# The first up products of a ConvFFN, made in the stage before it

## The chip, the cores and the metric

One core of one Trainium2 chip runs the whole kernel. The metric is the device time in microseconds (us); the median of three runs of the kernel before is 2347.77. The profile names the engines PE (TensorE, its matmuls), PEld (its weight loads), DVE (VectorE), ACT (ScalarE), POOL (GpSimd) and SP (SyncE). Each has its own queue of instructions, and they meet through semaphores.

## The reference, cut to what matters

One layer of a streaming encoder over 1024 prompt rows and 64 sample rows, width 1024, in float32. After attention and a gated merge come the two parts that this case is about:

```
x   = x + rms_norm(merged @ w_o, g_post_mix)
up  = rms_norm(x, g_pre_ffn) @ w_up                 # 1024 -> 2 x 2816, gate and value
buf = concatenate([conv_prev, up], axis=1)
conv = b_conv + sum(w_conv[i] * buf[:, i:i + t] for i in range(3))
gate, val = split(conv, 2)
x   = x + rms_norm((gelu(gate) * val) @ w_down, g_post_ffn)
```

## The kernel before

The kernel works in stages, each a function with a block of instructions for each engine. At the end of a stage all engines meet in a barrier, the stage's semaphores are cleared by POOL, a second barrier follows, and the next stage starts. Matrix products in float32 are made as three passes over high and low parts (`three_passes`, lines 166 to 170), so every operand is split first: a high part in a rounded type, and a low part that is the rest.

**The output stage** (`phase_output`) goes over nine tiles of rows, m = 0 to 8 (the ninth is the 64 sample rows). For a tile, PE makes `product(m)`, 48 matmuls into PSUM. ACT sums squares, DVE scales (`y_scaled`), adds x and writes `h2`, the normalized input of the FFN. PE turns h2 by eight transposes (`turn(m)`, line 1636). ACT then copies the high part of the result into `h2T` (named mergedT in the profile, line 1651) and DVE makes the low part (`lo(m)`, line 1689). Products run two tiles ahead of the transposes. DVE writes the low part of tile m - 2 within its work on tile m, and those of the last two tiles at the end. PSUM has eight banks: `p7_ps` takes four (two tiles), `p7_psT` the other four. POOL splits the first two pieces of w_up (gate and value, each 128 output features) early in this stage, into slots 0 and 1 of the weight ring.

**The FFN stage** (`phase_ffn`) has 22 steps f of 128 features. The 1092 columns of h2T (rows and gaps) are cut in three chunks of 364. In a step:

- PE: `up(f, b, 0)`, the gate half, three chunks of 24 matmuls; `down(f - 1)`, 54 matmuls in 18 shares; `up(f, b, 1)`, the value half. Step 0 has no down product. The first down product stands in step 1, between its gate and value halves. The chunks go to four banks of PSUM in turn.
- ACT: copies each chunk out of PSUM (line 1866, `up_taken`), begins the convolution of a half (line 1874), gelu (line 1879), and the high part of the hidden values (line 1881).
- DVE: adds the shares of the last step to the accumulator (line 1906), small copies (lines 1912 to 1914) and two multiply-adds for each half (line 1917), the product of gate and value (line 1933), the low part `hid_lo` (line 1935). `down` waits for `hid_lo`. At the stage's start it clears the accumulator (line 1942).
- POOL: splits the weights of the steps to come, n = 3f + kind (gate, value, w_down), a high part (line 148) and a low part (line 151). Six slots; a split of an up piece waits until the products that read the slot two steps before are made (line 1796).
- SP: loads the raw weights (line 142) into two buffers, one for even and one for odd n; a load waits until the split two before it is done.

Steps 0 and 1 are written out; the others run in a loop of 10 passes, two steps each.

Of the kernel before, what the change touches and what calls it, by code (L numbers as in the profile page):

```python
# [25 lines left out]
ACT = mybir.ActivationFunctionType  # L26
F32 = mybir.dt.float32
# [3 lines left out]
P = 128  # L31
D = 1024
KT = D // P
# [14 lines left out]
EPS = 1e-6  # L48
SCALE = DH ** -0.5
RSQRT_MAGIC = float(0x5F3759DF)  # L50


def rows(m):

    return P if m < TILES - 1 else DEC


def col(m):

    return GAP + m * P if m < TILES - 1 else SCOL  # L60
# [155 lines left out]
def build_layer(nc, a, o):  # L216

    base = (nc.sbuf_base + 63) // 64 * 64
    small = Place(nc, base, 3072)
    region = COLS * KT * 4 * 2  # L220
    r0 = base + 3072
    r1 = r0 + region
    rf = r1 + region
    f_size = nc.sbuf_usable_end - rf
    ident = small("ident", [P, P])
    par = small("par", [P, 512])
    d = Scratch(nc)
# [12 lines left out]
    phase_sample_attention(nc, a, d, ident, yaT, r1, region + f_size)  # L240
    phase_merge(nc, a, d, ybT, mgT, rf, f_size)
    ffn_place = Place(nc, rf, f_size)
    ffn_ring = Weights.buffers("p8", FFN_SLOTS, ffn_place, ffn_place)
    phase_output(nc, a, ident, mgT, d.x2, ffn_ring, r0, region, rf, f_size)
    phase_ffn(nc, a, o, ident, par, mgT, d.x2, ffn_ring, ffn_place.at, r0, region, rf, f_size)


def feature_part(nc, out, ring, slot, pair, chunk, first=0, count=3 * KT):
# [1292 lines left out]

def phase_output(nc, a, ident, mgT, x2_dram, ffn_ring, r0, r0_size, rf, rf_size):


    w_o = a["w_o"][0].rearrange("(k p) c -> p k c", p=P)
# [1 line left out]
    h2T = mgT  # L1549
    RAW = 4  # L1550
    LAG = 2
    with ExitStack() as ctx:
        s = Sems(nc, ctx, "p7")
# [3 lines left out]
        next_raw, next_hi, next_lo = ffn_ring  # L1557
# [16 lines left out]
        ss = f("p7_ss", [P, 2, 2])  # L1574
        rstd = f("p7_rstd", [P, 2, 2])
        tmp = f("p7_tmp", [P, 2, 2])
        ps = ctx.enter_context(nc.psum_tensor("p7_ps", [P, 2, D], F32))
        psT = ctx.enter_context(nc.psum_tensor("p7_psT", [P, 2, KT, P], F32))
        with nc.Block() as block:

            @block.sync
# [33 lines left out]
            @block.tensor  # L1615
            def _(pe):
                def product(m):
                    for c in range(2):
                        if m >= 2 and c == 0:
                            pe.wait_ge(s("y_scaled"), m - 1)  # L1620
                        for k in range(KT):
                            slot, at = 4 * c + k // 2, (k % 2) * 512
                            if m == 0 and k % 2 == 0:
                                pe.wait_ge(s("w_lo"), slot + 1)
                            last = three_passes(
                                nc, ps[0:rows(m), m % 2, c * 512:(c + 1) * 512], mgT[0][:, k, col(m):col(m) + rows(m)],
                                mgT[1][:, k, col(m):col(m) + rows(m)], w_hi[:, slot, at:at + 512],
                                w_lo[:, slot, at:at + 512], k == 0, k == KT - 1)
                    last.then_inc(s("product"), 1)

                def turn(m):
                    pe.wait_ge(s("h2_ready"), m + 1)
                    if m >= 2:
                        pe.wait_ge(s("h2T_lo"), m - 1)
                    for k in range(KT):
                        last = nc.tensor.transpose(psT[:, m % 2, k, 0:rows(m)], h2[0:rows(m), m % 2, k * P:(k + 1) * P],
                                                   ident[0:rows(m), 0:rows(m)])
                    last.then_inc(s("h2_turned"), 1)

                product(0)  # L1640
                product(1)
                for m in range(TILES):
                    if m + 2 < TILES:
                        product(m + 2)
                    turn(m)

            @block.scalar
            def _(act):
                def hi(m):
                    act.wait_ge(s("h2_turned"), m + 1)  # L1650
                    nc.scalar.activation(h2T[0][:, :, col(m):col(m) + rows(m)], psT[:, m % 2, :, 0:rows(m)],
                                         ACT.Copy).then_inc(s("h2T_hi"), 1)

                for n in range(8):
                    act.wait_ge(s(f"raw_ready{n % RAW}"), 16 * (n // RAW + 1))
                    nc.scalar.activation(w_hi[:, n, :], w_raw[n % RAW], ACT.Copy).then_inc(s("w_hi"), 1)
                act.wait_ge(s("ss_set"), 1)
                for m in range(TILES):
                    r = rows(m)
                    act.wait_ge(s("product"), m + 1)  # L1660
                    if m >= 2:
                        act.wait_ge(s("h2_ready"), m - 1)
                    nc.scalar.activation(junk[0:r, :], ps[0:r, m % 2, :], ACT.Square,
                                         accum_out=ss[0:r, m % 2, 0:1]).then_inc(s("squares"), 1)
                    act.wait_ge(s("squares"), 2 * m + 1)
                    if m >= LAG:
                        hi(m - LAG)
                    act.wait_ge(s("x2_ready"), m + 1)
                    nc.scalar.activation(junk[0:r, :], y[0:r, m % 2, :], ACT.Square,
                                         accum_out=ss[0:r, m % 2, 1:2]).then_inc(s("squares"), 1)  # L1670
                    act.wait_ge(s("squares"), 2 * m + 2)
                for m in range(TILES - LAG, TILES):
                    hi(m)

            @block.vector
            def _(dve):
# [9 lines left out]
                def lo(m):  # L1686
                    c = slice(col(m), col(m) + rows(m))
                    dve.wait_ge(s("h2T_hi"), m + 1)
                    nc.vector.tensor_tensor(h2T[1][:, :, c], psT[:, m % 2, :, 0:rows(m)], h2T[0][:, :, c].bitcast(F32),
                                            ALU.subtract).then_inc(s("h2T_lo"), 1)  # L1690

                for m in range(TILES):
# [5 lines left out]
                    nc.vector.scalar_tensor_tensor(out=y[0:r, b, :], in0=ps[0:r, b, :], scalar=rstd[0:r, b, 0:1],  # L1698
                                                   in1=g_post[0:r, :], op0=ALU.mult, op1=ALU.mult).then_inc(s("y_scaled"), 1)
                    dve.wait_ge(s("y_scaled"), m + 1)  # L1700
                    dve.wait_ge(s(f"x_ready{b}"), 16 * (m // 2 + 1))
# [11 lines left out]

def phase_ffn(nc, a, o, ident, par, h2T, x2_dram, ffn_ring, ffn_ring_end, r0, r0_size, rf, rf_size):

# [10 lines left out]
    with ExitStack() as ctx:  # L1728
# [18 lines left out]
        psU = ctx.enter_context(nc.psum_tensor("p8_psU", [P, BANKS, 512], F32))  # L1747
# [18 lines left out]
        with nc.Block() as block:  # L1766
# [25 lines left out]
            def _(pool):  # L1792
                def step(f, b, first):
                    for kind in range(AHEAD if first else 0, 3):
                        if kind < 2:
                            pool.wait_ge(s("up"), f * CHUNKS + (kind + 1) * NCH)
                        else:
                            pool.wait_ge(s("share"), f * SHARES + SHARES)
                        n = 3 * b + kind

                        ring.split_one(pool, f * 3 + kind, (f - b) * 3 // 2 + n // 2, n, n % 2)
# [14 lines left out]
            def _(pe):  # L1816
# [23 lines left out]
                                         ring.lo[:, slot, w], True, True).then_inc(s("share"), 1)  # L1840

                def step(f, b, first):
                    up(f, b, 0)
                    if not first:
                        down(f - 1, 1 - b)
                    up(f, b, 1)

                pe.sem_inc(s("up"), 2 * CHUNKS)
# [8 lines left out]
            @block.scalar  # L1857
            def _(act):
                def step(f, b, first):
                    for kind in range(2):  # L1860
                        for c in range(NCH):
                            n = kind * NCH + c
# [14 lines left out]
                        if kind == 0:  # L1877
                            act.wait_ge(s("conv"), f * 2 + 3)
                            nc.scalar.activation(cv[0][:, GAP:COLS], cv[0][:, GAP:COLS], ACT.Gelu_apprx_tanh).then_inc(s("gelu"), 1)  # L1879
                    act.wait_ge(s("hid"), f + 2)  # L1880
                    nc.scalar.activation(hid_hi[:, GAP:COLS], cv[0][:, GAP:COLS], ACT.Copy).then_inc(s("hid_hi"), 1)

                act.sem_inc(s("up_taken"), BANKS)  # L1883
# [106 lines left out]
```

## Time and profile before

| | |
|---|---|
| three runs | 2345.87, 2347.77, 2348.48 us |
| the profiled execution, its own time | 2350.03 us |
| its span, first to last instruction | 2348.1 us |
| mean granted TensorE clock | 0.961 of full speed |
| PE busy | 2163.6 us, 92% |
| DVE, ACT, POOL busy | 1306.8, 746.6, 858.4 us |
| PE busy in 1393.00 to 1491.35 (output stage) | 98.35 of 98.35 us, clock 1.00 |
| PE busy in 1491.35 to 1504.17 | 1.11 of 12.82 us, clock 0.70 |
| PE busy in 1504.17 to 1542.77 (up products of steps 0 and 1) | 38.59 of 38.60 us, clock 0.92 |
| PE busy in 1542.77 to 2295.10 | 752.33 of 752.33 us, clock 1.00 |

Times in the profile are microseconds from the start of the span. A busy share is that of an engine's own instructions; the matmuls overlap, so that one of 0.33 us can follow another after 0.17 us. In a timeline, the bracket at the end of a line tells how long the engine had been idle and which instruction released it.

### The profile page before, as it was taken

The page shows a single profiled execution, that of the slowest core. Times are in us where ns is not written, and L with a number is a line of the kernel's source. Part 1 is how long each engine was busy: PE and PEld are TensorE (multiplying, and loading weights), DVE is VectorE, ACT ScalarE, POOL GpSimd, SP SyncE. Part 2 cuts the span into 40 slices and gives each one's busy share as a digit, 9 for nine tenths or more (in the row PEclk, how much of TensorE's full clock was granted, in tenths as well). Part 3 has the DMA queues.
Part 4 walks back from the last instruction along what each step waited for, and adds up shares of the span by engine and source line. Part 5 has one row for each costly group of instructions (what it writes and reads, how often), then busy time and mean ns, then how long its engine had stood idle before and what let it go on. Part 6 is the DMA issues. An engine that isn't in the chain of part 4 may idle for free. (4 is left out here: it accounts for less than half of the span.)

```text
span 2348.1 us, 33627 instructions
## 1 busy us (share of the span) xinstructions
PE 2163.6 (92%) x12884; PEld 2056.2 (88%) x12884; DVE 1306.8 (56%) x1719; ACT 746.6 (32%) x1429; POOL 858.4 (37%) x485
## 2 busy tenths in 40 slices
PE   6999999995999999937996989899999999999993
PEld 6999999995999999927996978699999999999992
DVE  5054220001787788745563547666767667677666
ACT  3211102232677777723432122221121211212122
POOL 2335334442555455432543310324233242332404
PEclk9999999998999999968997989899999999999996
DMA  5124224456555554346645443211111111111104
GB/s 169 46 83 145 84 75 160 160 162 169 131 129 133 144 128 124 77 140 165 173 136 183 122 151 95 81 45 46 36 54 36 45 47 33 54 44 36 45 0 162
DMA packets 289092, 237.39 MB, mean 101 GB/s; under 512 B 50950, under 2 KB 265430, under 8 KB 288982
## 3 DMA queue, kind: packets, MB, share of 16 engines
q1 hardware_dynamic: 280240, 222.24, 33.0%
q10 hardware_dynamic: 7510, 9.19, 1.3%
q0 software_dynamic: 1232, 4.46, 0.5%
q8 instruction: 74, 1.21, 0.2%
q14 instruction: 36, 0.29, 0.0%
HBM read 168.51 MB, written 67.33 MB: 100 GB/s over the span
## 5 line engine op out<-in xcount | busy, mean ns | idle before, releaser
L148 POOL TENSOR_SCALAR p_w_hi<-p_w_raw 128x1024 fp32r<-128x1024 f32 x136 | 167.7, 1233 | 896.0 <-PE p_psD L170 418.5
L995 DVE TENSOR_TENSOR_SCAN p_rest<-p_rest 128x896 f32<-128x896 f32 (+7 forms) x128 | 218.5, 1718 | 304.2 <-ACT p_rest L947 303.5
L151 POOL TENSOR_TENSOR p_w_lo<-p_w_raw,p_w_hi 128x1024 fp32r<-128x1024 f32 x136 | 356.7, 2622 | 11.3
L168 PE MATMUL p_psU<-mergedT_lo,p_w_hi 128*128 128x364 f32 x1056 | 347.1, 329 | 2.7 <-ACTq L1883 2.7
L170 PE MATMUL p_psU<-mergedT_hi,p_w_lo 128*128 128x364 f32 x1056 | 347.9, 329 | 0.0
L169 PE MATMUL p_psU<-mergedT_hi,p_w_hi 128*128 128x364 f32 x1056 | 347.5, 329 | 0.0
L257 PE MATMUL p_psB<-hT_lo,p_w_hi 128*128 128x364 f32 x960 | 318.8, 332 | 2.4 <-issue 2.4
L257 PE MATMUL p_psB<-hT_hi,p_w_lo 128*128 128x364 f32 x960 | 316.5, 330 | 0.0
L257 PE MATMUL p_psB<-hT_hi,p_w_hi 128*128 128x364 f32 x960 | 315.9, 329 | 0.0
L1906 DVE TENSOR_TENSOR p_acc<-p_psD,p_acc 128x512 f32<-128x512 f32 (+1 forms) x396 | 273.4, 691 | 46.6 <-PE p_psD L170 45.3
L823 POOL TENSOR_TENSOR p_weights<-p_weights,p_rest 128x895 f32<-128x895 f32 (+7 forms) x128 | 159.8, 1254 | 200.5 <-DVE p_rest L995 198.6
L168 PEld LDWEIGHTS p_psU<-mergedT_lo,p_w_hi 128*128 128x128 f32 x1056 | 199.3, 189 | 5.0 <-POOLq L132 2.9
L169 PEld LDWEIGHTS p_psU<-mergedT_hi,p_w_hi 128*128 128x128 f32 x1056 | 199.3, 189 | 0.8
L170 PEld LDWEIGHTS p_psU<-mergedT_hi,p_w_lo 128*128 128x128 f32 x1056 | 199.2, 189 | 0.0
L257 PEld LDWEIGHTS p_psB<-hT_lo,p_w_hi 128*128 128x128 f32 x960 | 181.4, 189 | 3.2 <-issue 2.6
L532 ACT ACTIVATE p_line<-p_psB 128x364 f32<-128x364 f32 x117 | 55.5, 474 | 403.1 <-PE p_psB L257 403.1
L257 PEld LDWEIGHTS p_psB<-hT_hi,p_w_hi 128*128 128x128 f32 x960 | 181.2, 189 | 0.0
L257 PEld LDWEIGHTS p_psB<-hT_hi,p_w_lo 128*128 128x128 f32 x960 | 181.1, 189 | 0.0
L168 PE MATMUL p_psD<-p_w_lo,p_hid_hi 128*128 128x512 f32 (+1 forms) x396 | 156.5, 395 | 9.4 <-issue 9.4
L169 PE MATMUL p_psD<-p_w_hi,p_hid_hi 128*128 128x512 f32 (+1 forms) x396 | 157.1, 397 | 0.0
L170 PE MATMUL p_psD<-p_w_hi,p_hid_lo 128*128 128x512 f32 (+1 forms) x396 | 156.3, 395 | 0.0
L1879 ACT ACTIVATE p_conv_gate<-p_conv_gate 128x1090 f32<-128x1090 f32 x22 | 24.6, 1117 | 367.5 <-DVE p_conv_gate L1917 367.5
(208 smaller groups left out, 4364.5 us busy)
## 6 DMA issues: line engine op xcount, KB each, us to landing
p_w_raw<-in_w_up SPq DMA_DIRECT2D x44, 512.0 KB, 3.8
p_w_raw<-in_w_in SPq DMA_DIRECT2D x40, 512.0 KB, 4.0
p_w_raw<-in_w_down SPq DMA_DIRECT2D x22, 512.0 KB, 3.5
p_kT_hi<-k_hi_scratch SPq DMA_DIRECT2D x32, 256.0 KB, 4.5
p_kT_lo<-k_lo_scratch SPq DMA_DIRECT2D x32, 256.0 KB, 5.1
p_w_raw<-in_w_gate SPq DMA_DIRECT2D x16, 512.0 KB, 4.1
p_raw_k<-in_cache_sb_k SPq DMA_DIRECT2D x8, 1024.0 KB, 7.9
p_raw_v<-in_cache_sb_v SPq DMA_DIRECT2D x8, 1024.0 KB, 6.7
```

Of the source, the lines that this page charges most:

```text
L148: self.nc.gpsimd.tensor_scalar(self.hi[:, slot, :], self.raw[:, parity, :], 1.0, 0.0, ALU.mult, ALU.add).then_inc(self.split, 1)
L151: self.nc.gpsimd.tensor_tensor(self.lo[:, slot, :], self.raw[:, parity, :], self.hi[:, slot, :].bitcast(F32), ALU.subtract).then_inc(self. ...
L168: nc.tensor.matmul(out, stat_hi, mov_lo, start=first, stop=False)
L169: nc.tensor.matmul(out, stat_hi, mov_hi, start=False, stop=False)
L170: return nc.tensor.matmul(out, stat_lo, mov_hi, start=False, stop=last)
L257: last = nc.tensor.matmul(out[:, 0:CH], stat[:, slot, w], mov[:, k, c], start=(at == 0), stop=(at == 3 * KT - 1))
L532: nc.scalar.activation(line_of(n)[:, c * CH:(c + 1) * CH], psB[:, q % 3, 0:CH], func).then_inc(s("line"), 1)
L823: nc.gpsimd.tensor_tensor(wt[:, b % 6, 0:n - 1], wt[:, b % 6, 0:n - 1], rest[:, b % 4, 1:n], ALU.mult).then_inc(s("weights"), 1)
L995: nc.vector.tensor_tensor_scan(src, src, src, 1.0, ALU.mult, ALU.bypass).then_inc(s("scanned"), 1)
L1879: nc.scalar.activation(cv[0][:, GAP:COLS], cv[0][:, GAP:COLS], ACT.Gelu_apprx_tanh).then_inc(s("gelu"), 1)
L1906: nc.vector.tensor_tensor(acc[0:r, m, w], psD[0:r, share_bank(b, n), :], acc[0:r, m, w], ALU.add).then_inc(s("added"), 1)
```

## The change

PE makes four of the six up chunks of step 0 in the output stage. In `UP_FIRST` the chunks of step 0 get an order of their own: gate 0, gate 1, value 0, value 1, then gate 2, value 2. The first two are made ahead of the transposes of the last tile, the next two behind them. They write into a PSUM tensor `ps_up` of four banks that both stages share: in the output stage its banks 0 and 1 are the product's second buffer, banks 2 and 3 the transposes' second buffer. The early chunks therefore wait: the first two for `y_scaled` of tile 7, the other two for the low part of tile 7. The FFN stage starts with a count of four chunks made, makes the last two, and ACT begins the convolutions of both halves of step 0 only behind the sixth copy. POOL's wait for the gate slot becomes one for the fifth chunk of two steps before, in place of the third, in every step. The semaphore that tells that the early chunks are made has a group of its own, which is given back behind the FFN stage.

```diff
+UP_FIRST = [(0, 0), (0, 1), (1, 0), (1, 1), (0, 2), (1, 2)]
+UP_EARLY = 4
...
+    with ExitStack() as both:
+        early = Sems(nc, both, "early")
+        ps_up = both.enter_context(nc.psum_tensor("ps_up", [P, 4, 512], F32))
...
-        ps = ctx.enter_context(nc.psum_tensor("p7_ps", [P, 2, D], F32))
-        psT = ctx.enter_context(nc.psum_tensor("p7_psT", [P, 2, KT, P], F32))
+        ps = [ctx.enter_context(nc.psum_tensor("p7_ps", [P, D], F32)), ps_up[:, 0:2, :].rearrange("p b c -> p (b c)")]
+        psT = [ctx.enter_context(nc.psum_tensor("p7_psT", [P, KT, P], F32)), ps_up[:, 2:4, :].rearrange("p b (k c) -> p (b k) c", c=P)]
...
+                def up(n):
+                    kind, c = UP_FIRST[n]
+                    pe.wait_ge(s("next_split"), 2 * kind + 2)
+                    pe.wait_ge(s("h2T_lo"), 3 * c + 3)
+                    if n < 2:
+                        pe.wait_ge(s("y_scaled"), TILES - 1)
+                    else:
+                        pe.wait_ge(s("h2T_lo"), TILES - 1)
+                    cols = slice(c * CH, (c + 1) * CH)
+                    for k in range(KT):
+                        w = slice(k * P, (k + 1) * P)
+                        last = three_passes(nc, ps_up[:, n, 0:CH], next_hi[:, kind, w], next_lo[:, kind, w],
+                                            h2T[0][:, k, cols], h2T[1][:, k, cols], k == 0, k == KT - 1)
+                    last.then_inc(early("up_opened"), 1)
...
                     if m + 2 < TILES:
                         product(m + 2)
+                    if m == TILES - 1:
+                        up(0)
+                        up(1)
                     turn(m)
+                for n in range(2, UP_EARLY):
+                    up(n)
...
-                            pool.wait_ge(s("up"), f * CHUNKS + (kind + 1) * NCH)
+                            pool.wait_ge(s("up"), f * CHUNKS + (CHUNKS - 1, CHUNKS)[kind])
...
                 def step(f, b, first):
+                    if first:
+                        pe.wait_ge(early("up_opened"), UP_EARLY)
+                        pe.sem_inc(s("up"), UP_EARLY)
+                        for n in range(UP_EARLY, CHUNKS):
+                            kind, c = UP_FIRST[n]
+                            pe.wait_ge(s("up_taken"), n + 1)
...
+                            last.then_inc(s("up"), 1)
+                        return
...
+                def first_step():
+                    for n, (kind, c) in enumerate(UP_FIRST):
+                        act.wait_ge(s("up"), n + 1 + 2 * CHUNKS)
+                        if c == 0:
+                            act.wait_ge(s("conv"), kind + 1)
+                        nc.scalar.activation(x[kind][:, c * CH:(c + 1) * CH], psU[:, n % BANKS, 0:CH], ACT.Copy).then_inc(s("up_taken"), 1)
+                    act.wait_ge(s("up_taken"), CHUNKS + BANKS)
+                    act.wait_ge(s("hid_lo"), 1)
+                    act.wait_ge(s("hid"), 1)
+                    for kind in range(2):
+                        at = kind * FT
+                        nc.scalar.activation(cv[kind][:, GAP:COLS], x[kind][:, GAP:COLS], ACT.Identity,
+                                             scale=par[:, PAR["w_conv2"] + at:PAR["w_conv2"] + at + 1],
+                                             bias=par[:, PAR["b_conv"] + at:PAR["b_conv"] + at + 1]).then_inc(s("conv_begun"), 1)
+                    act.wait_ge(s("conv"), 3)
+                    nc.scalar.activation(cv[0][:, GAP:COLS], cv[0][:, GAP:COLS], ACT.Gelu_apprx_tanh).then_inc(s("gelu"), 1)
+                    act.wait_ge(s("hid"), 2)
+                    nc.scalar.activation(hid_hi[:, GAP:COLS], cv[0][:, GAP:COLS], ACT.Copy).then_inc(s("hid_hi"), 1)
```

## Rows read from the trace of the kernel before

**Rows 1.** PE's waits from 1480 us on: us in total, times, longest.

```profile
PE p_psD L168 <- issue: 9.4, 1, 9.4
PE p_psT L1636 <- DVE p_h L1709: 9.0, 1, 9.0
PE p_psU L168 <- ACTq L1883: 2.7, 1, 2.7
```

**Rows 2.** Busy us of each engine in a stretch, clock, DMA.

```profile
1567.00:2295.00 728.00, 728.00 (x3963) 674.33 (x3961) 505.56 (x600) 144.72 (x200) 227.77 (x112) 1.00 0.13 39
```

**Rows 3.** PE's timeline: start, us, instruction, [idle before, releaser].

```profile
1489.44 1.91 PE L1636 MATMUL p_psT<-ident,p_h 128*128 128x128 f32 x16
...
1500.34 1.11 PE L1636 MATMUL p_psT<-ident,p_h 64*128 64x64 f32 x8 [8.99 <-DVE p_h L1709]
1504.17 0.65 PE L168 MATMUL p_psU<-mergedT_lo,p_w_hi 128*128 128x364 f32 x1 [2.72 <-ACTq L1883]
...
1542.77 0.39 PE L168 MATMUL p_psD<-p_w_lo,p_hid_hi 128*128 128x512 f32 x1
```

**Rows 4.** DVE's timeline at the end of the output stage.

```profile
1500.21 1.21 DVE L1689 TENSOR_TENSOR mergedT_lo<-p_psT,mergedT_hi 128x1024 fp32r<-128x1024 f32 x1
1502.12 0.69 DVE L1689 TENSOR_TENSOR mergedT_lo<-p_psT,mergedT_hi 128x512 fp32r<-128x512 f32 x1 [0.70 <-ACT mergedT_hi L1651]
```

**Rows 5.** Busy us in two stretches (columns as in rows 2).

```profile
1504.10:1510.10 6.00, 5.92 (x20) 5.96 (x21) 4.09 (x1) 0.00 (x0) 2.46 (x2) 0.50 0.58 175
...
2295.10:2304.50 9.40, 0.00 (x0) 0.00 (x0) 5.72 (x7) 2.88 (x3) 0.00 (x0) 0.68 0.84 318
```

**Rows 6.** ACT's timeline, step 0 of the FFN.

```profile
1515.09 0.47 ACT L1866 ACTIVATE p_up_gate<-p_psU 128x364 f32<-128x364 f32 x1 [3.52 <-PE p_psU L170]
1519.06 0.48 ACT L1866 ACTIVATE p_up_gate<-p_psU 128x364 f32<-128x364 f32 x1 [3.50 <-PE p_psU L170]
1519.57 1.30 ACT L1874 ACTIVATE p_conv_gate<-p_up_gate,par 128x1090 f32<-128x1090 f32 x1
```

**Rows 7.** PE's queue, two lines that open the FFN: duration ns, first and last start.

```profile
L1848 PEldq EVENT_SEMAPHORE  x1: 51/51/51, 1503.7 to 1503.7; - x1
...
L1821 PEldq EVENT_SEMAPHORE  x1: 51/51/51, 1504.1 to 1504.1; - x1
```

**Rows 8.** POOL's timeline, first splits of the FFN.

```profile
1507.55 1.04 POOL L148 TENSOR_SCALAR p_w_hi<-p_w_raw 128x1024 fp32r<-128x1024 f32 x1 [11.14 <-DMA p_w_raw<-in_w_down]
...
1512.15 2.39 POOL L151 TENSOR_TENSOR p_w_lo<-p_w_raw,p_w_hi 128x1024 fp32r<-128x1024 f32 x1
1515.09 1.05 POOL L148 TENSOR_SCALAR p_w_hi<-p_w_raw 128x1024 fp32r<-128x1024 f32 x1 [0.55 <-issue]
...
1531.20 1.05 POOL L148 TENSOR_SCALAR p_w_hi<-p_w_raw 128x1024 fp32r<-128x1024 f32 x1 [3.20 <-PE p_psU L170]
```

**Rows 9.** DVE's timeline, value half and low split of step 0.

```profile
1534.94 2.75 DVE L1917 SCALAR_TENSOR_TENSOR p_conv_val<-p_up_val,par,p_conv_val 128x1090 f32<-128x1090 f32 x2
...
1540.27 1.29 DVE L1935 TENSOR_TENSOR p_hid_lo<-p_conv_gate,p_hid_hi 128x1090 fp32r<-128x1090 f32 x1 [1.18 <-ACT p_hid_hi L1881]
```

**Rows 10.** DVE's timeline near 1593 us.

```profile
1593.39 3.33 DVE L1917 SCALAR_TENSOR_TENSOR p_conv_gate<-p_up_gate,par,p_conv_gate 128x1090 f32<-128x1090 f32 x1 [0.15 <-DVE p_up_gate L1914]
1596.87 1.90 DVE L1917 SCALAR_TENSOR_TENSOR p_conv_gate<-p_up_gate,par,p_conv_gate 128x1090 f32<-128x1090 f32 x1 [0.15 <-DVE p_conv_gate L1917]
```

**Rows 11.** POOL's timeline near 1593 us.

```profile
1593.17 2.40 POOL L151 TENSOR_TENSOR p_w_lo<-p_w_raw,p_w_hi 128x1024 fp32r<-128x1024 f32 x1
1595.54 2.09 POOL L148 TENSOR_SCALAR p_w_hi<-p_w_raw 128x1024 fp32r<-128x1024 f32 x1
1597.71 3.32 POOL L151 TENSOR_TENSOR p_w_lo<-p_w_raw,p_w_hi 128x1024 fp32r<-128x1024 f32 x1
```

**Rows 12.** SP's timeline: the loads behind the boundary.

```profile
1504.17 7.29 SPq L142 DMA_DIRECT2D p_w_raw<-in_w_up  x2
```

**Rows 13.** The last release of semaphores: first and last start.

```profile
L87 POOLq DRAIN  x1: 107/107/107, 2347.5 to 2347.5; - x1
```

More of the change, by code:

```diff
@@ L243, in build_layer @@
     ffn_ring = Weights.buffers("p8", FFN_SLOTS, ffn_place, ffn_place)
[L244 to L245 removed]
+    with ExitStack() as both:
+        early = Sems(nc, both, "early")
+        ps_up = both.enter_context(nc.psum_tensor("ps_up", [P, 4, 512], F32))
+        phase_output(nc, a, ident, mgT, d.x2, ffn_ring, early, ps_up, r0, region, rf, f_size)
+        phase_ffn(nc, a, o, ident, par, mgT, d.x2, ffn_ring, early, ps_up, ffn_place.at, r0, region, rf, f_size)
 def feature_part(nc, out, ring, slot, pair, chunk, first=0, count=3 * KT):
@@ L1540, in _, with phase_output @@
                 lo(len(ORDER) - 1)
-def phase_output(nc, a, ident, mgT, x2_dram, ffn_ring, r0, r0_size, rf, rf_size):
+def phase_output(nc, a, ident, mgT, x2_dram, ffn_ring, early, ps_up, r0, r0_size, rf, rf_size):
     w_o = a["w_o"][0].rearrange("(k p) c -> p k c", p=P)
@@ L1625, in product @@
                             last = three_passes(
-                                nc, ps[0:rows(m), m % 2, c * 512:(c + 1) * 512], mgT[0][:, k, col(m):col(m) + rows(m)],
+                                nc, ps[m % 2][0:rows(m), c * 512:(c + 1) * 512], mgT[0][:, k, col(m):col(m) + rows(m)],
                                 mgT[1][:, k, col(m):col(m) + rows(m)], w_hi[:, slot, at:at + 512],
@@ L1635, in turn @@
                     for k in range(KT):
-                        last = nc.tensor.transpose(psT[:, m % 2, k, 0:rows(m)], h2[0:rows(m), m % 2, k * P:(k + 1) * P],
+                        last = nc.tensor.transpose(psT[m % 2][:, k, 0:rows(m)], h2[0:rows(m), m % 2, k * P:(k + 1) * P],
                                                    ident[0:rows(m), 0:rows(m)])
                     last.then_inc(s("h2_turned"), 1)
+                def up(n):
[12 more added lines that the diff above has]
+                    last.then_inc(early("up_opened"), 1)
                 product(0)
@@ L1650, in hi @@
                     act.wait_ge(s("h2_turned"), m + 1)
-                    nc.scalar.activation(h2T[0][:, :, col(m):col(m) + rows(m)], psT[:, m % 2, :, 0:rows(m)],
+                    nc.scalar.activation(h2T[0][:, :, col(m):col(m) + rows(m)], psT[m % 2][:, :, 0:rows(m)],
                                          ACT.Copy).then_inc(s("h2T_hi"), 1)
@@ L1662, in _ @@
                         act.wait_ge(s("h2_ready"), m - 1)
-                    nc.scalar.activation(junk[0:r, :], ps[0:r, m % 2, :], ACT.Square,
+                    nc.scalar.activation(junk[0:r, :], ps[m % 2][0:r, :], ACT.Square,
                                          accum_out=ss[0:r, m % 2, 0:1]).then_inc(s("squares"), 1)
@@ L1688, in lo @@
                     dve.wait_ge(s("h2T_hi"), m + 1)
-                    nc.vector.tensor_tensor(h2T[1][:, :, c], psT[:, m % 2, :, 0:rows(m)], h2T[0][:, :, c].bitcast(F32),
+                    nc.vector.tensor_tensor(h2T[1][:, :, c], psT[m % 2][:, :, 0:rows(m)], h2T[0][:, :, c].bitcast(F32),
                                             ALU.subtract).then_inc(s("h2T_lo"), 1)
@@ L1697, in _ @@
                         dve.wait_ge(s(f"x2_stored{b}"), 16 * (m // 2))
-                    nc.vector.scalar_tensor_tensor(out=y[0:r, b, :], in0=ps[0:r, b, :], scalar=rstd[0:r, b, 0:1],
+                    nc.vector.scalar_tensor_tensor(out=y[0:r, b, :], in0=ps[b][0:r, :], scalar=rstd[0:r, b, 0:1],
                                                    in1=g_post[0:r, :], op0=ALU.mult, op1=ALU.mult).then_inc(s("y_scaled"), 1)
@@ L1712, in _, with phase_ffn @@
                     lo(m)
-def phase_ffn(nc, a, o, ident, par, h2T, x2_dram, ffn_ring, ffn_ring_end, r0, r0_size, rf, rf_size):
+def phase_ffn(nc, a, o, ident, par, h2T, x2_dram, ffn_ring, early, ps_up, ffn_ring_end, r0, r0_size, rf, rf_size):
     w_up = a["w_up"][0].rearrange("(k p) c -> p k c", p=P)
@@ L1746, in phase_ffn @@
         junk = nc.alloc_sbuf_tensor_at("p8_squares", [P, D], F32, offset=r1 + (TILES + 1) * D * 4)
-        psU = ctx.enter_context(nc.psum_tensor("p8_psU", [P, BANKS, 512], F32))
+        psU = ps_up
         psD = ctx.enter_context(nc.psum_tensor("p8_psD", [P, BANKS, 512], F32))
@@ L1842, in step @@
                 def step(f, b, first):
+                    if first:
[4 more added lines that the diff above has]
+                            pe.wait_ge(s("up_taken"), n + 1)
+                            cols = slice(c * CH, (c + 1) * CH)
+                            for k in range(KT):
+                                w = slice(k * P, (k + 1) * P)
+                                last = three_passes(nc, psU[:, n % BANKS, 0:CH], ring.hi[:, kind, w], ring.lo[:, kind, w],
+                                                    h2T[0][:, k, cols], h2T[1][:, k, cols], k == 0, k == KT - 1)
+                            last.then_inc(s("up"), 1)
+                        return
                     up(f, b, 0)
-                    if not first:
-                        down(f - 1, 1 - b)
+                    down(f - 1, 1 - b)
                     up(f, b, 1)
@@ L1859, in step @@
                 def step(f, b, first):
+                    if first:
+                        first_step()
+                        return
                     for kind in range(2):
```

## The prediction, made before the run

> **What bounds the kernel now.** I read the busy shares first. TensorE (PE) is busy 92% of the span, so a gain has to be a shorter stretch of PE. I then asked for PE's own waits behind the 1480 us mark. There are only three: 9.0 us for the normalized rows of the last tile at the end of the output stage, 2.7 us across the boundary of the two stages, and 9.4 us before the last down product [rows 1]. Between 1567 and 2295 us PE has no idle time and full clock [rows 2]. So the steps of the FFN after the first two are set by PE alone, and the change can earn only what it takes out of the stretch from the last transposes of the output stage to the first down product. Everything behind that product moves with it.
>
> In PE's timeline that stretch goes so: 16 transposes end at 1491.35; PE idles to 1500.34; 8 transposes of the last tile end at 1501.45; the first up product starts at 1504.17; the first down product at 1542.77 [rows 3]. The stage ends when VectorE (DVE) has split the last tile at 1502.81 [rows 4]. That is 1.36 us before PE starts. The clock was at its lower level (0.50, so 1.2 GHz) from 1504.10 to 1510.10: 20 matmuls in 6.0 us, 0.30 us each [rows 5]. At full clock a chunk of 24 takes 1519.06 - 1515.09 = 3.97 us, by ScalarE's (ACT's) copies [rows 6], so 0.165 us each, and the lower level cost 20 x 0.135 = 2.7 us. The reader is to see 8.99 idle, 2.72 idle and 2.7 of clock: some 14 us that PE work could fill or warm.
>
> **What the change moves on PE.** No matmul is added or removed. up(0) and up(1) wait for y_scaled of tile 7 and the splits of tiles 2 and 5, all long done when turn(7) ends. They take 2 x 3.97 from 1491.1 to 1499.1, wholly in the idle stretch. turn(8) still starts at 1500.34, because its input comes from DVE at that time. up(2) and up(3) need the low part of tile 7, ready at 1500.21 + 1.21 = 1501.42 [rows 4]. They run from 1501.5 to 1509.5, the last one ending at 1509.65. Now PE, and not DVE, closes the output stage: with the 0.8 us from 1502.81 to the barrier's release near 1503.6 (PE's first instruction behind it is at 1503.7 [rows 7]) the release comes at 1510.45, **6.85 us later than before**. That delays every other engine: two weight loads of SP, GpSimd's (POOL's) splits, DVE's memset of the accumulator, ACT's copies.
>
> PE in the FFN has two up chunks left of step 0. The fifth needs a free bank, so it waits until ACT has copied the first. PE's opening semaphore instructions are about 0.17 us apart (three from 1503.7 to 1504.1 [rows 7]); with two more of them ACT starts some 0.7 after the release and copies in 0.47, and PE starts 1.3 after it, at 1511.75. Chunks five and six take 8.0, to 1519.8. Then the gate product of step 1 needs its split weights. On POOL's queue two splits come first: w_down of step 0 and w_up of step 1, 1507.55 to 1514.54 before [rows 8], 1514.4 to 1521.4 now. PE waits 1.7 us, runs three chunks (11.95) and is done at 1533.45. If nothing else were late the down product would start there, 9.3 us earlier than before.
>
> **What is late next: hid_lo of step 0.** The down product needs it. Before, it came at 1540.27 + 1.30 = 1541.57 [rows 9], 1.2 us ahead of PE, and that margin is all that hid it. Its chain now starts when ACT has copied chunk six: copy at 1520.0, +0.51 to the first convolution pass, +1.30 for it [rows 6], so DVE starts at 1521.9. Six long DVE operations follow: two multiply-adds for the gate half, two for the value half, the product and the low split; between product and split ACT makes the high part (1.17 us). Alone, a multiply-add takes 2.75 / 2 = 1.37 and the split 1.29, as I take for the product [rows 9]; small copies add 0.35 a half: 1521.9 + 2 x 3.1 + 1.3 + 1.17 + 1.3 = 1531.9, under PE's 1533.45.
>
> But they aren't alone. At 1593 us both engines have work, and they take turns: DVE's multiply-add, asked for at 1593.39, ends 1596.72, that is 1.15 behind the end of POOL's low split (1595.57); POOL's next high split, asked for at 1595.54, ends 0.91 behind that; the second multiply-add 1.14 behind the high split; POOL's low split 2.26 behind it [rows 10, 11]. So an operation waits for the whole of one of the other's: 0.95 for a high split, 2.27 for a low one, 1.15 for DVE's. The Trainium skill (SBUF — State Buffer, Who interferes with whom) states the rule: GpSimd and a VectorE operation with two SBUF inputs share a port pair, whoever issues first holds it for the whole instruction. The trace agrees; by the rule the sum is the one worked out below from rows, without it the 1531.9 above.
>
> In the kernel before, POOL stood still during most of this chain, as it waited for the value product (3.20 us idle before 1531.20 [rows 8]). Now all of its waits for PE up to the split of step 2's value weights (n = 7) are met by 1519.8, so it is limited by its loads alone. A load is issued when the split two before it is done, and its own split starts 4.0 later (two issues of 0.37 end at 1504.17 + 7.29 = 1511.46, so the second was made at 1511.1; split at 1515.09 [rows 8, 12]). n = 4 starts at 1521.95, n = 5 and 6 find their data there. DVE asks for its first multiply-add at 1521.9 + 0.35 = 1522.25, 0.3 after POOL. From there the two alternate without a hole: four high and four low splits (n = 4 to 7) and six DVE operations. 1521.95 + (1.05 + 3 x 0.95) + 4 x 2.27 + 6 x 1.15 = 1541.8; with handover gaps **1542.0**. The last low split gets in ahead of hid_lo, because POOL asks 1.0 after the product's end and DVE 1.17. Down starts at 1542.05, 0.7 before 1542.77.
>
> **Two small terms.** A second semaphore group is given back at the very end: one more drain, clear and barrier like the one from 2347.5 to 2348.1 [rows 13]: +0.6. And PE now idles 1533.6 to 1542.05, 8.4 us. Gaps of that size lose the clock: in the 9.4 us before the last down product it is 0.68 on average [rows 5]. No row prices a cold start here in the down product; the bounds are 0 and 3.3 (7 us at half, the longest I take), and I take the 2.7 lost at 1504. The Trainium skill (TensorE: Matmul & The Clock Gate, key terms) prices it as throttled time x (1 - K/N): 6.0 x 0.5 = 3.0, with which the sum would be 0.3 higher.
>
> Sum: -0.7 + 0.6 + 2.7 = **+2.6 us**, so 2350.0 -> 2352.6 against the profiled execution's own time. That execution was 2.3 above the median of the runs, so for the median 2347.8 -> 2350.3. The work that hides moved splits later (POOL's changed wait, which in all later steps moves the gate split from the end of a down product to the fifth up chunk) is PE's unbroken stream [rows 2]; I cost it at nothing, and DVE's gate half then meets less of POOL.
>
> **Rivals.**
> 1. *DVE is first at 1522.* Then its multiply-add goes ahead of n = 4, and n = 7 falls behind hid_lo: 1.05 + 2.27 less, down at 1538.8. A difference of 0.3 us in a load or in PE's start decides. PE's gap is then 5.1; the half clock may or may not come. -3.9 + 0.6 + (0 to 2.7): 2344.5 to 2347.2, centre 2346.5.
> 2. *The handovers don't bite* (POOL is later, or the port is shared): down follows PE at 1533.45 with no cold clock: -9.3 + 0.6 = -8.7, 2339.1; with half of them 2343. For it: 14 us of idle and cold time are real. Against: [rows 10, 11].
> 3. *Slower: the changed POOL wait.* It holds in every step. The gate split of two steps on now starts at the fifth chunk (some 1563.5 on the old scale, where it started 1559.2), ends at 1567.1, and the value split can't start before 1567.6; that one ends in front of DVE's copy of the next chain, which has 1.2 us of margin to PE. If the pair runs over 0.5 + 1.2 us, each further microsecond is paid in 10 passes of the loop: at 1 us, +10, 2358. Against it: DVE is idle in that stretch, so nothing blocks POOL there.
>
> **How the numbers follow.** A measurement of this kernel can tell about 0.2% (4.7 us) from no change. Forecast 0.47, rival 1 0.27, rival 2 0.17, rival 3 0.09. Faster by over 0.2%: rival 2 and the edge of rival 1, 0.20; slower: rival 3 and a long cold clock, 0.10; within: 0.70. The range goes from rival 2's half (2342) to the forecast with 3.3 of clock loss and 2 us of late release (2353). The forecast's own range is 2348.5 to 2352.
>
> **What would show it.** Right: up products filling 1491 to 1499 at full clock; the release near 1510.4; a wait of some 1.7 us for weights near 1520; PE idle for 8 us in front of the first down product, its releaser DVE's hid_lo; POOL splits back to back from 1522 to 1541, with DVE operations of 2 to 3.4 us between them; a clock of 0.5 behind that gap. Wrong: that gap under 3 us, which makes rival 2; a new PE wait inside the loop, which makes rival 3.

## The result, and the profile after

The changed kernel takes 2351.78 us (median of 16 runs, 2350.06 to 2353.94) against 2347.22 (16 runs): ratio **1.0019, 95% interval [1.0011, 1.0027]**, so 4.6 us slower. Forecast were 2.6 us more, within 0.2% at 0.70. The range (2342 to 2353) holds the time.

First PE's waits in the changed kernel from 1480 us on, in the columns of [rows 1]. Lines have moved in the file: 168 to 170 are now 170 to 172, and the FFN's PSUM tensor is called ps_up.

```profile
PE p_psD L170 <- issue: 19.1, 2, 9.7
PE ps_up L170 <- ACT p_up_gate L1929: 2.0, 1, 2.0
PE ps_up L170 <- POOL p_w_lo L153: 1.5, 1, 1.5
PE p_psT L1641 <- DVE p_h L1735: 1.0, 1, 1.0
PE ps_up L170 <- DVE mergedT_lo L1715: 0.5, 1, 0.5
```

The idle 9.0 us ahead of the last tile's transposes have become 1.0. In place of it and of the 2.7 us at the boundary stand 0.5, 2.0 and 1.5 us, and a second wait of the long kind: 9.7 us ahead of the first down product (the line with "issue", for which the profile names no releaser, holds it and the known 9.4). PE's timeline, against [rows 3]:

```profile
1496.87 0.71 PE L1641 MATMUL p_psT<-ident,p_h 64*128 64x64 f32 x8 [1.02 <-DVE p_h L1735]
1498.09 0.41 PE L170 MATMUL ps_up<-mergedT_lo,p_w_hi 128*128 128x364 f32 x1 [0.51 <-DVE mergedT_lo L1715]
...
1509.86 0.43 PE L170 MATMUL ps_up<-mergedT_lo,p_w_hi 128*128 128x364 f32 x1 [1.98 <-ACT p_up_gate L1929]
1519.65 0.43 PE L170 MATMUL ps_up<-mergedT_lo,p_w_hi 128*128 128x364 f32 x1 [1.54 <-POOL p_w_lo L153]
1541.55 0.77 PE L170 MATMUL p_psD<-p_w_lo,p_hid_hi 128*128 128x512 f32 x1 [9.70 <-issue]
```

The place where the two kernels begin to differ is not at the same time in all executions: the last tile's transposes start at 1500.34 in the one before, at 1496.87 here, and between 1496 and 1500 in the runs below, whichever kernel it is. So I count from the start of those transposes. From there to the first down product the kernel before took 42.4 us (1542.77 - 1500.34), this one **44.7**. From the first down product to the last one it was 761.8 (1542.77 to 2304.54); now it is 764.4 (to 2305.95). From there to the end 43.5, now 44.8. That is +2.25, +2.6 and +1.3, together 6.2 us, where the medians say 4.6 with an interval of 2.6 to 6.3. One execution of each is compared here. The first of the three stretches repeats in the runs below whose edits should leave its length alone (42.3 us in run 3, 45.0 in run 2); the starting place scatters by some microseconds.

DVE's chain of step 0 in the changed kernel:

```profile
1520.05 0.99 DVE L1972 COPY p_tails<-p_up_gate 128x2 f32<-128x2 f32 x1 [1.07 <-ACT p_conv_gate L1935]
...
1521.21 5.49 DVE L1977 SCALAR_TENSOR_TENSOR p_conv_gate<-p_up_gate,par,p_conv_gate 128x1090 f32<-128x1090 f32 x2
1526.62 2.37 DVE L1972 COPY p_tails<-p_up_val 128x2 f32<-128x2 f32 x1
...
1528.97 1.03 DVE L1974 COPY p_up_val<-par 128x2 f32<-128x2 f32 x1
1530.04 5.59 DVE L1977 SCALAR_TENSOR_TENSOR p_conv_val<-p_up_val,par,p_conv_val 128x1090 f32<-128x1090 f32 x2
1535.74 3.23 DVE L1993 TENSOR_TENSOR p_conv_gate<-p_conv_gate,p_conv_val 128x1090 f32<-128x1090 f32 x1
1540.15 1.29 DVE L1995 TENSOR_TENSOR p_hid_lo<-p_conv_gate,p_hid_hi 128x1090 fp32r<-128x1090 f32 x1 [1.18 <-ACT p_hid_hi L1941]
```

and POOL's splits n = 4 to 7 in the same stretch:

```profile
1519.97 1.05 POOL L150 TENSOR_SCALAR p_w_hi<-p_w_raw 128x1024 fp32r<-128x1024 f32 x1 [0.38 <-issue]
1521.10 2.39 POOL L153 TENSOR_TENSOR p_w_lo<-p_w_raw,p_w_hi 128x1024 fp32r<-128x1024 f32 x1
1523.46 2.10 POOL L150 TENSOR_SCALAR p_w_hi<-p_w_raw 128x1024 fp32r<-128x1024 f32 x1
1525.64 3.31 POOL L153 TENSOR_TENSOR p_w_lo<-p_w_raw,p_w_hi 128x1024 fp32r<-128x1024 f32 x1
1528.93 1.05 POOL L150 TENSOR_SCALAR p_w_hi<-p_w_raw 128x1024 fp32r<-128x1024 f32 x1
1530.06 2.37 POOL L153 TENSOR_TENSOR p_w_lo<-p_w_raw,p_w_hi 128x1024 fp32r<-128x1024 f32 x1
1532.99 1.50 POOL L150 TENSOR_SCALAR p_w_hi<-p_w_raw 128x1024 fp32r<-128x1024 f32 x1 [0.55 <-DMA p_w_raw<-in_w_up]
1534.57 3.25 POOL L153 TENSOR_TENSOR p_w_lo<-p_w_raw,p_w_hi 128x1024 fp32r<-128x1024 f32 x1
```

The two lists are to be read side by side. A copy of two columns takes 2.37 us: it is asked for at 1526.62 and ends with POOL's low split at 1528.95. The pair of multiply-adds takes 5.5 us, twice, where it took 2.75 alone [rows 9]. The product takes 3.23, where it takes 1.29 in run 1 below. POOL pays too: 2.10 and 3.31 in place of 1.05 and 2.39. hid_lo is there at 1541.44, and PE starts 0.1 us later. The profile does not name hid_lo as the releaser; that it is what PE waited for is read from these two times and from run 1.

The clock in three stretches (columns as in [rows 2]): the second early pair of chunks, the first shares of the first down product, and the same behind the last wait:

```profile
1499.47:1502.88 3.41, 3.41 (x14) 3.41 (x13) 0.00 (x0) 0.00 (x0) 0.00 (x0) 0.52 0.02 5
1541.55:1547.25 5.70, 5.70 (x14) 4.51 (x15) 2.28 (x4) 1.29 (x1) 0.00 (x0) 0.51 0.00 0
...
2305.95:2311.80 5.85, 5.85 (x14) 4.61 (x15) 2.43 (x4) 1.15 (x2) 0.90 (x1) 0.51 0.95 341
```

The second row was expected, the first was not: PE had been idle for only 1.0 and 0.5 us before it, with eight small transposes between. The last is no part of the change: the kernel before has such a stretch there as well, which lasted 4.3 us.

### The profile page after: what moved, and what is told of

It reads as the page before. It is cut to its first block and busy times, and to the rows that moved or that the text cites. A ratio compares the mean times of both kernels' runs of the same rounds, so it can differ in the third digit from the quotient of the medians.

```text
span 2350.8 us, 33646 instructions
## 1 busy us (share of the span) xinstructions
PE 2163.8 (92%) x12884; PEld 2054.8 (87%) x12884; DVE 1303.2 (55%) x1719; ACT 748.4 (32%) x1429; POOL 822.8 (35%) x485
## 5 line engine op out<-in xcount | busy, mean ns | idle before, releaser
L150 POOL TENSOR_SCALAR p_w_hi<-p_w_raw 128x1024 fp32r<-128x1024 f32 x136 | 148.4, 1091 | 937.3 <-PE p_psD L172 416.9
L170 PE MATMUL ps_up<-mergedT_lo,p_w_hi 128*128 128x364 f32 x1056 | 346.8, 328 | 4.0 <-ACT p_up_gate L1929 2.0
L172 PE MATMUL ps_up<-mergedT_hi,p_w_lo 128*128 128x364 f32 x1056 | 347.5, 329 | 0.0
L171 PE MATMUL ps_up<-mergedT_hi,p_w_hi 128*128 128x364 f32 x1056 | 347.1, 329 | 0.0
L153 POOL TENSOR_TENSOR p_w_lo<-p_w_raw,p_w_hi 128x1024 fp32r<-128x1024 f32 x136 | 340.5, 2504 | 11.3
L170 PEld LDWEIGHTS ps_up<-mergedT_lo,p_w_hi 128*128 128x128 f32 x1056 | 198.9, 188 | 6.9 <-ACT p_up_gate L1929 2.3
L171 PEld LDWEIGHTS ps_up<-mergedT_hi,p_w_hi 128*128 128x128 f32 x1056 | 198.7, 188 | 0.8
L172 PEld LDWEIGHTS ps_up<-mergedT_hi,p_w_lo 128*128 128x128 f32 x1056 | 198.9, 188 | 0.0
```

The source lines that it names most:

```text
L150: self.nc.gpsimd.tensor_scalar(self.hi[:, slot, :], self.raw[:, parity, :], 1.0, 0.0, ALU.mult, ALU.add).then_inc(self.split, 1)
L153: self.nc.gpsimd.tensor_tensor(self.lo[:, slot, :], self.raw[:, parity, :], self.hi[:, slot, :].bitcast(F32), ALU.subtract).then_inc(self. ...
L170: nc.tensor.matmul(out, stat_hi, mov_lo, start=first, stop=False)
L171: nc.tensor.matmul(out, stat_hi, mov_hi, start=False, stop=False)
L172: return nc.tensor.matmul(out, stat_lo, mov_hi, start=False, stop=last)
```

## Experiments

In all of these, "before" is the kernel before on the same chip. Ratios are to it.

**1. POOL kept off the port.** Only the first of POOL's splits that meet DVE's chain waits:

```diff
                         n = 3 * b + kind
+                        if isinstance(f, int) and f == 1 and kind == 1:
+                            pool.wait_ge(s("hid_lo"), 2)
                         ring.split_one(pool, f * 3 + kind, ...)
```

> The changed kernel with one wait added: POOL makes its splits from n = 4 on only when hid_lo of step 0 is made, so that nothing on POOL meets DVE's chain of step 0. Theory (the turns that DVE and POOL take on the shared port hold hid_lo back, and the idle gap that follows costs clock): the first down product starts some 23 us behind the release of the FFN stage and not 33, PE's gap of 9.7 us goes or is under 1.5 us, no lower clock behind it: 9.6 + 2.6 = 12 us less than the changed kernel, near 2340, ratio 0.997 to the kernel before. Rival (the late release and the late loads alone set the down product): no change, 2352. Rival (POOL's changed wait costs in every step of the loop): no change either.

Measured: 2341.66 us, ratio 0.9972 [0.9961, 0.9983]; the changed kernel's own ratio is 1.0019, so 4.7 thousandths or 11 us below it. DVE's chain in this run:

```profile
1522.38 0.17 DVE L1973 COPY p_tails<-p_up_gate 128x2 f32<-128x2 f32 x1 [1.20 <-ACT p_conv_gate L1936]
...
1522.72 2.74 DVE L1978 SCALAR_TENSOR_TENSOR p_conv_gate<-p_up_gate,par,p_conv_gate 128x1090 f32<-128x1090 f32 x2
...
1525.72 2.74 DVE L1978 SCALAR_TENSOR_TENSOR p_conv_val<-p_up_val,par,p_conv_val 128x1090 f32<-128x1090 f32 x2
1528.57 1.29 DVE L1994 TENSOR_TENSOR p_conv_gate<-p_conv_gate,p_conv_val 128x1090 f32<-128x1090 f32 x1
1531.05 1.30 DVE L1996 TENSOR_TENSOR p_hid_lo<-p_conv_gate,p_hid_hi 128x1090 fp32r<-128x1090 f32 x1 [1.18 <-ACT p_hid_hi L1942]
```

The chain takes 9.97 us (1522.38 to 1532.35) in place of 21.4 (1520.05 to 1541.44). PE goes from the gate product of step 1 into the down product with no gap, at 1534.03, that is 34.9 us behind the transposes and not 44.7. Its only wait behind that is the one of 9.4 us before the last down product. The release and the first loads came as late as in the changed kernel, so the rival that these set the down product is refuted. So is the rival that POOL's changed wait is the loss: it is still in this kernel. The theory's 12 us were 11.

**2. The gap filled.** 54 matmuls with no reader, ahead of the first down product:

```diff
                     up(f, b, 0)
+                    if isinstance(f, int) and f == 1:
+                        for _ in range(54):
+                            nc.tensor.matmul(psD[:, 3, 0:CH], ring.hi[:, 3, 0:P], h2T[0][:, 0, 0:CH], start=True, stop=True)
                     down(f - 1, 1 - b)
```

> The changed kernel with 54 more matmuls of 364 columns on PE ahead of the first down product (9.0 us at full clock; they write a PSUM bank that the down product overwrites). They fill the idle gap, no more. Theory (of the loss, 2.6 us are the lower clock behind the gap): the down product starts where it did, and the shares behind it run at full clock: 2.6 us less than the changed kernel, near 2349.2, ratio 1.0008 to the kernel before. Rival (the clock behind the gap costs nothing, since DVE's additions or hid_lo set the pace there): no change, 2351.8. Rival (filler delays the down product): slower than 2352.

Measured: 2350.01 us, ratio 1.0011 [1.0001, 1.0020]. That is 1.9 us under the changed kernel's ratio, but the intervals overlap, so the time alone doesn't settle it. The trace does:

```profile
1531.37 9.16 PE L1885 MATMUL p_psD<-mergedT_hi,p_w_hi 128*128 128x364 f32 x54
1541.48 0.47 PE L170 MATMUL p_psD<-p_w_lo,p_hid_hi 128*128 128x512 f32 x1 [0.95 <-issue]
```

and, for the stretch behind it,

```profile
1541.48:1547.20 5.72, 5.72 (x25) 4.68 (x26) 4.74 (x7) 1.29 (x1) 0.00 (x0) 1.00 0.00 0
```

25 matmuls at clock 1.00, where the changed kernel made 14 at 0.51. From the first down product to the last it is 761.8 us (1541.48 to 2303.31), as in the kernel before. The lower clock behind the gap costs 2.6 us, and the gap itself is left as it was.

**3. POOL's changed wait alone**, in the kernel before:

```diff
-                            pool.wait_ge(s("up"), f * CHUNKS + (kind + 1) * NCH)
+                            pool.wait_ge(s("up"), f * CHUNKS + (CHUNKS - 1, CHUNKS)[kind])
```

> The kernel before with one line of the change alone: POOL's split of a gate piece waits for the fifth up chunk of two steps before, in place of the third, in all steps. Theory: hidden by PE's unbroken stream, 2347.2 within 1 us; in the trace the gate half's multiply-adds (5.5 us for the two before) get shorter, and PE keeps no wait in the loop. Rival (this wait is the loss): 4.5 us slower, 2351.7, with a new wait of PE or a late hid_lo in each pass.

Measured: 2348.22 us, ratio 1.0001 [0.9992, 1.0010]. PE's waits are those of [rows 1], to a tenth. POOL in the first loop pass:

```profile
1554.06 1.05 POOL L148 TENSOR_SCALAR p_w_hi<-p_w_raw 128x1024 fp32r<-128x1024 f32 x1 [20.98 <-PE p_psD L170]
1555.19 2.39 POOL L151 TENSOR_TENSOR p_w_lo<-p_w_raw,p_w_hi 128x1024 fp32r<-128x1024 f32 x1
1561.96 1.05 POOL L148 TENSOR_SCALAR p_w_hi<-p_w_raw 128x1024 fp32r<-128x1024 f32 x1 [4.38 <-PE p_psU L170]
1563.09 2.38 POOL L151 TENSOR_TENSOR p_w_lo<-p_w_raw,p_w_hi 128x1024 fp32r<-128x1024 f32 x1
1565.99 1.05 POOL L148 TENSOR_SCALAR p_w_hi<-p_w_raw 128x1024 fp32r<-128x1024 f32 x1 [0.52 <-PE p_psU L170]
```

The gate split starts at 1561.96 and takes its undisturbed 1.05 and 2.38; the value split follows 0.5 us behind it, as worked out for rival 3. The median multiply-add of the gate half goes from 1.97 to 1.36 us, and none of it reaches the end, because PE sets the pace. Rival 3 is refuted.

**4. Two early chunks.** Gate 0 and gate 1 only, both ahead of the transposes; ACT's and POOL's code as before:

```diff
-UP_FIRST = [(0, 0), (0, 1), (1, 0), (1, 1), (0, 2), (1, 2)]
-UP_EARLY = 4
+UP_FIRST = [(0, 0), (0, 1), (0, 2), (1, 0), (1, 1), (1, 2)]
+UP_EARLY = 2
```

> Two early chunks in place of four, gate 0 and gate 1, both ahead of the last tile's transposes; the other four in the FFN stage in the old order, with ACT's and POOL's old instructions. The release of the FFN stage isn't moved. Theory: the gate half's convolution is made while PE makes the value half, POOL's splits n = 5 to 7 still meet the value half. Worked out in the trace of the kernel before: PE done with the gate product of step 1 at 1532.3, hid_lo at 1535.6, down at 1535.7 against 1542.8; with 0.6 us for the second release of semaphores 6.5 us less than before, 2340.7, ratio 0.9972. Rival (any early chunk costs as much as it gives, by cold clock or by the shared PSUM banks): 2347 or more.

Measured: 2345.24 us, ratio 0.9988 [0.9979, 0.9997]: faster than both, but 2.9 us and not 6.5. Its chain still meets POOL (columns as before):

```profile
1522.83 5.48 DVE L1955 SCALAR_TENSOR_TENSOR p_conv_val<-p_up_val,par,p_conv_val 128x1090 f32<-128x1090 f32 x2
1528.42 3.29 DVE L1971 TENSOR_TENSOR p_conv_gate<-p_conv_gate,p_conv_val 128x1090 f32<-128x1090 f32 x1
1532.88 1.29 DVE L1973 TENSOR_TENSOR p_hid_lo<-p_conv_gate,p_hid_hi 128x1090 fp32r<-128x1090 f32 x1 [1.18 <-ACT p_hid_hi L1919]
```

PE waits 2.1 us for it, and the clock was lower once more behind that: 18 matmuls at 0.70 from 1534.28 to 1540.00. The clock is what the forecast of this run left out, here and at the start of the stage (22 matmuls in 6.4 us).

**5 and 6. Two early chunks, POOL held; then also no second group of semaphores.** Run 5 is run 4 with the edit of run 1. Run 6 gives the early chunks' semaphore to the output stage:

```diff
-        early = Sems(nc, both, "early")
...
-                    last.then_inc(early("up_opened"), 1)
+                    last.then_inc(s("up_opened"), 1)
...
                 for n in range(2, UP_EARLY):
                     up(n)
+                pe.wait_ge(s("up_opened"), UP_EARLY)
```

> The kernel with two early chunks (run e4_two) and POOL held from n = 4 on until hid_lo of step 0 is made. In e4_two PE waited 2.1 us for hid_lo and the clock fell once more behind it (1.6 us). Theory (the port's turns cause both): both go, 3.7 us less than e4_two, near 2341.5, ratio 0.9972; the down product follows the gate product of step 1 without a gap. Rival (hid_lo is late because the value half starts late): no change against e4_two, 2345.2.

> As e5_two_hold, and the semaphore that tells that the early chunks are made belongs to the output stage, where PE waits for it before it leaves the stage: no second group is given back at the end. Theory: 0.8 us less (from the last store's landing to the end 0.74 us, as in the kernel before, in place of 1.58), near 2340.7, ratio 0.9969; the time alone can't tell this from e5_two_hold, the end of the trace can. Rival (PE's wait at the stage's end costs as much): 2341.5.

Measured: 2340.46 us, ratio 0.9970 [0.9958, 0.9982], and 2339.08 us, 0.9963 [0.9949, 0.9976]. In both PE goes into the down product without a gap and at clock 1.00. The intervals of run 4 and run 5 touch (0.9979 and 0.9982), but the slowest of run 5 (2341.94) is under the fastest of run 4 (2343.63). That the turns held run 4 back is shown; the rival expected no change. Not all of the difference is theirs. The down product came 36.6 us behind the transposes in run 4 (1497.72 to 1534.28) and 32.8 in run 5 (1499.58 to 1532.35). Of these 3.8 us, 2.1 are the wait that went; most of the rest is a shorter stretch of lower clock at the stage's start, 2.85 us in run 5 where run 4 had some 6.4, though no edit was made there. In run 5:

```profile
1503.12:1505.97 2.85, 2.85 (x9) 2.85 (x10) 0.97 (x1) 0.82 (x2) 0.00 (x0) 0.51 0.76 241
```

The intervals of runs 5 and 6 overlap, so the time doesn't settle what run 6 adds. What run 6 removed is seen at the end of the trace. POOL's queue, the lines that give semaphores back, first of the changed kernel and then of run 6:

```profile
L89 POOLq DRAIN  x3: 53/65/83, 2349.3 to 2350.0; - x3
L89 POOLq EVENT_SEMAPHORE_RANGE_CLEAR  x3: 44/91/134, 2349.4 to 2350.1; - x3
```

```profile
L89 POOLq DRAIN  x1: 107/107/107, 2336.8 to 2336.8; - x1
L89 POOLq EVENT_SEMAPHORE_RANGE_CLEAR  x1: 197/197/197, 2336.9 to 2336.9; - x1
```

In the changed kernel 1.5 us lie between the first of these and the end (2350.8), in run 6 0.6, as before (2347.5 to 2348.1).

**7. The clock kept up in the output stage.** Run 6 with matmuls that have no reader around the last tile's transposes:

```diff
                         up(0)
                         up(1)
+                        pe.wait_ge(s("y_scaled"), TILES)
+                        fill(5)
                     turn(m)
+                fill(8)
```

> As e6_best, with matmuls whose result nobody reads around the last tile's transposes in the output stage: 5 in PE's gap of 1.0 us ahead of them, 8 (1.3 us) in the gap of 2.8 us behind them. Theory (a gap of 1 us, 0.7 us of small transposes and another gap together let the clock fall, and the third up chunk pays for it at half rate): no clock of 0.50 at the start of the FFN stage, about 2.4 us less than e6_best, near 2338.3, ratio 0.9959. Rival (the clock falls all the same, or the filler delays the stage's end): 2340.7 or more.

Measured: 2336.65 us, ratio 0.9952 [0.9938, 0.9965]. The intervals of run 6 and run 7 overlap, but the slowest of run 7 (2337.07) is under the fastest of run 6 (2338.99), and the traces differ. Run 6 and run 7 at the start of the FFN stage:

```profile
1501.17:1506.90 5.73, 5.73 (x19) 5.73 (x20) 3.86 (x1) 0.82 (x2) 2.30 (x2) 0.50 0.61 186
```

```profile
1499.91:1527.86 27.95, 27.95 (x169) 27.95 (x169) 17.00 (x14) 9.45 (x13) 9.55 (x6) 1.00 0.25 77
```

19 matmuls in 5.73 us at 0.50 against a whole way to the down product at 1.00. From the transposes to the down product run 6 took 34.0 us (1497.76 to 1531.73), run 7 31.5 (1496.37 to 1527.86): 2.5 us, where 2.4 were expected; the medians are 2.4 apart. Single executions differ, though. In the trace of run 5, whose code around the last tile's transposes is run 6's, the lower clock lasted half as long, and against its 32.8 us run 7 gains 1.3. This is the fastest version, 0.48% under the kernel before.

**8. The same in the changed kernel** (fill(5) ahead of the transposes, fill(2) behind them):

> The changed kernel with matmuls whose result nobody reads: 5 in the gap of 1.0 us ahead of the last tile's transposes, 2 in the gap of 0.5 us behind them. Theory (the clock of 0.50 that stood over the last two early chunks for 3.4 us, and which the prediction's sum left out, comes from these two gaps): no such clock, up(2) and up(3) take 8.1 us and not 9.8, the FFN stage starts 1.7 us earlier: 1.7 us less than the changed kernel, near 2350.5, ratio 1.0010. Rival (the clock falls there whatever PE does): no change, 2352.2.

Measured: 2352.20 us, ratio 1.0021 [1.0012, 1.0030]: no gain. The clock stayed up over all the early chunks, but fell after the next gap instead:

```profile
1495.50:1506.30 10.80, 10.62 (x66) 9.70 (x64) 3.11 (x4) 0.60 (x1) 0.00 (x0) 1.00 0.01 2
1508.30:1513.30 5.00, 5.00 (x21) 5.00 (x22) 3.64 (x1) 1.04 (x3) 2.01 (x2) 0.66 0.68 210
1540.39:1544.10 3.71, 3.71 (x9) 2.98 (x10) 1.38 (x2) 1.29 (x1) 0.00 (x0) 0.55 0.00 0
```

The first half of the expectation holds: the FFN's first up product starts 11.4 us behind the transposes (1496.88 to 1508.30) where it was 13.0 (1496.87 to 1509.86). But the stretch at half clock moved into the stage, behind a gap of 2.0 us, and from the transposes to the down product it is 43.5, 1.2 less than in the changed kernel. In the medians even that isn't seen. The profiled execution took 2350.08 us, 2.1 under the median of its run, so its trace doesn't tell what the others did; why the median shows no gain stays open.

## Why the prediction was right, and where its terms were off

**The mechanism is as forecast, and the number is partly luck.** The early chunks fill the idle stretch; PE closes the output stage and the release comes late; hid_lo is what is late next; DVE and POOL take turns on their port; PE idles over 8 us, and the clock is at its lower level behind it. Run 1 removes the turns and with them the loss, run 2 the clock alone, run 3 clears the only part of the change that acts in the loop. PE's smaller waits came out at 1.98 and 1.54 us, for 2.1 and 1.7. The clock behind the gap cost 2.63 (764.40 - 761.77) for 2.7. That term was taken from another stretch, and such stretches lasted from 2.85 us (run 5) to some 6.4 (run 4), so a hit this close is luck. The sum's first term is what failed: the down product was to start 0.7 us earlier than before, counted from the last tile's transposes, and it started 2.25 later. The terms as measured add up to 6.2 us and not 2.6. The medians differ by 4.6, which is nearer to the forecast than its terms are.

**The release was mis-sized.** "up(2) and up(3) ... run from 1501.5 to 1509.5": 8.0 us at full clock. They took 9.8 (1498.09 to 1507.87), because the clock was at 0.52 over 3.4 us. The sum had taken a gap of 1 us for harmless. SP's first load came 12.1 us behind the transposes, forecast 10.3. This is +1.8 of the +3.0 by which the down product came later than forecast (44.7 against 1542.05 - 1500.34 = 41.7 us).

**The order of the turns was half right.** "From there the two alternate without a hole": four high and four low splits in front of hid_lo. All eight did run ahead of it, but in another order. DVE's two-column copies used up turns: the first was held until 1528.95, the third behind POOL's next high split, and then the multiply-add behind the low one. So POOL got two operations in a row, and its last low split (1534.57 to 1537.82) stood ahead of the product, not between the product and hid_lo. Up to the product's end the sum still held: eight splits and five long DVE operations took 19.0 us (1519.97 to 1538.97) for 18.9 in the forecast. Behind it ACT's pass, which the forecast had hidden behind the low split, lay open: 2.47 us from the product's end to hid_lo's, where the forecast had 1.15 for hid_lo. n = 4 started 0.3 us sooner behind the first load than forecast. So the chain from SP's first load to hid_lo took 32.45 us (1508.99 to 1541.44) for 31.4, which is +1.05 of the rest.

**Small terms.** The second group of semaphores: 0.9 (1.5 against 0.6, above) for 0.6; drain, two clears and the barrier come once more. The remaining 0.4 us behind the last down product goes with its own stretch of lower clock, 5.9 us long and not 4.3; no run ties that to the change.

**The rivals.** DVE first at the port: no, POOL's high split started at 1519.97, 1.2 us ahead of the first multiply-add. Handovers that don't bite: no; run 1 shows what it would have been, 2341.7. Its forecast of 2339.1 lacked the 1.8 us of late release. The changed wait: no (run 3).

**The turns and the clock, beside the stated rules.** The Trainium skill (SBUF — State Buffer, Who interferes with whom) states that the second to issue is fully blocked for the whole instruction. The trace agrees for operations with two inputs, in both directions: DVE's product took 3.23 us for 1.29, and POOL's high split 2.10 for 1.05 behind a multiply-add. With both engines ready, these traces show turns. The two-column copy has one input and was held as well (0.17 us in run 1, 2.37 here). The Trainium skill (TensorE: Matmul & The Clock Gate, Terms) prices lower clock at throttled time x (1 - K/N). Its estimate for the stretch behind the gap ahead of the down product is 5.7 x 0.5 = 2.85 us; measured 2.63.

## What to carry to other kernels

Work moved from behind a stage's boundary to in front of it is only free in the idle time that it fills: two of the four chunks fitted, and with them alone the kernel gained; the other two moved the release of five engines. Once GpSimd was held off, four early chunks (run 1, 0.9972) and two (run 5, 0.9970) came out alike, so no gain of the other two is seen. When a chain on VectorE becomes the next to be waited for, look at what GpSimd has ready in that stretch; a single wait that keeps GpSimd off, where its results aren't needed yet, was worth 11 us here. After an edit that leaves short PE gaps, read the granted clock in the microseconds behind them, not only the gaps.

## What the runs showed of the hardware

- The clock went to its lower level after short gaps. With idle stretches of 1.0 and 0.5 us around eight small transposes, it was at 0.52 from 1499.47 to 1502.88, though PE was busy again from 1498.09. With 1.0 and 2.7 us (run 6) it was lower for 5.7 us behind the second, with 1.0 and 2.8 (run 5) for 2.85. With 0.2 and 1.3 us (run 7) it did not fall.
- Taking such a gap away need not take the lower clock away: in run 8 it came after the next gap, of 2.0 us, for some 3.4 us.
- VectorE and GpSimd, both with work, alternate. A multiply-add of 1090 columns costs the other 1.15 us, a high split of 1024 costs 0.95 and a low split 2.3; a copy of two columns takes a turn like a long one, and took up to 2.37 us. VectorE's memset of the accumulator (1511.22 to 1518.96 in the changed kernel) took no turns: the four split operations that ran beside it took 1.05, 2.41, 1.04 and 2.37 us, as alone.
